# A two-layer streaming encoder: filling products in pieces behind the key tiles, and a second attention that goes tile by tile

## The reference

```python
# layer 0
a_out = gmlp_spatial_gate(...)                      # 1024 wide
b_out = dsa_attention(q, k, v, iq, ik, iw, bias)    # 16 heads of 64, one shared k and v,
                                                    # top-256 keys of those allowed, softmax
mix   = concat([a_out, b_out]) @ w_out              # 2048 x 1024
# layer 1
c_out_heads = swa_sink_attention(q, k, v, sinks, bias)  # 16 heads, 2 key/value heads (8 each),
                                                        # band of two 64-token chunks, sink logit
mix   = c_out_heads @ c_w_out                       # 1024 x 1024
# both layers
h = h + rms_norm(mix, g1)
h = h + rms_norm(squared_relu_mlp(rms_norm(h, g2)), g3)
```

## Time and profile before

| what | value |
|---|---|
| median of 3 runs (from to) | 2545.99 us (2543.73 to 2550.15) |
| span of the profiled execution | 2557.9 us (no other time of that execution is given) |
| TensorE busy | 95% |
| first attention, first to last denominators | 463.18 to 805.51 us |
| second attention, first to last denominators | 1684.85 to 1843.71 us |
| first product of the stage after it | 1910.08 us |

### The profile page before, as it was taken

One profiled execution on the slowest core, in us unless ns is written; L12 is line 12 of the kernel. 1 busy time (PEld: TensorE's weight loads), 2 busy tenths in 40 slices (PEclk: granted clock), 3 DMA queues, 4 the chain that ended last, 5 costly groups with the idle time before them and its releaser, 6 DMA issues.

```text
span 2557.9 us, 34068 instructions
## 1 busy us (share of the span) xinstructions
PE 2427.4 (95%) x11680; PEld 1996.4 (78%) x11680; DVE 1694.0 (66%) x2859; ACT 1183.7 (46%) x2025; POOL 1472.5 (58%) x817
## 2 busy tenths in 40 slices
PE   7899999898998999999999999989989999999997
PEld 5689888777776778888778887867777888878886
DVE  5469998667775486655666676167758655576676
ACT  5442533556664274444333236265555444434331
POOL 2111578645553129887678642357725887578951
PEclk9999999899999999999999999989999999999999
DMA  5380643733544624455644444755553454754343
GB/s 150 63 129 26 134 101 125 238 103 100 157 131 163 214 86 140 140 168 151 238 165 162 141 134 128 169 148 136 133 186 99 146 167 138 240 199 146 115 140 132
DMA packets 324244, 369.64 MB, mean 145 GB/s; under 512 B 13874, under 2 KB 222290, under 8 KB 322052
## 3 DMA queue, kind: packets, MB, share of 16 engines
q1 hardware_dynamic: 315476, 351.96, 47.2%
q10 hardware_dynamic: 8352, 15.21, 2.0%
q0 software_dynamic: 272, 0.62, 0.1%
HBM read 237.18 MB, written 130.55 MB: 144 GB/s over the span
## 4 chain that ended last, share of the span: by engine, by line
PE 75%; DVE 6%; POOL 6%; DMA 4%; issue 4%; ACT 4%; SPq 1%; POOLq 0%; DVEq 0%; ACTq 0%
PE ps L462 72%; PE ps L2675 2%; POOL attn_out_split L1239 1%; POOL attn_out L1237 1%; DMA hidden<-cat_scratch 1%; DMA cat_scratch<-attn_out_split 1%; ACT relu_scores L1508 1%; DVE masks L2068 1%; POOL w_split L417 1%; PE ps L579 1%; DMA h_operand_raw<-h_operand_scratch 1%; POOL attn_out_split L1235 1%; DVE logits L2202 1%; ACT junk L1349 1%; POOL attn_out_low L1232 1%
## 5 line engine op out<-in xcount | busy, mean ns | idle before, releaser
L462 PE MATMUL ps<-xn_T,w_split 128*128 128x512 f32 (+1 forms) x2928 | 679.7, 391 | 2.2 <-ACT x_sums L1386 1.4
L462 PEld LDWEIGHTS ps<-xn_T,w_split 128*128 128x128 f32 (+1 forms) x2928 | 548.6, 188 | 121.2 <-DVE xn_T L2001 2.7
L417 POOL TENSOR_TENSOR w_split<-w_raw,w_split 128x1024 fp32r<-128x1024 f32 x78 | 199.5, 2568 | 484.4 <-ACT w_split L410 484.0
L462 PE MATMUL ps<-w_operand,h_operand 128*128 128x512 f32 x2016 | 461.6, 391 | 11.4 <-DVE acc L2471 7.5
L462 PEld LDWEIGHTS ps<-w_operand,h_operand 128*128 128x128 f32 x2016 | 379.8, 189 | 93.2 <-issue 10.7
L1263 POOL TENSOR_TENSOR w_split<-w_raw,w_split 128x512 fp32r<-128x512 f32 x168 | 242.2, 1454 | 105.5 <-ACT w_split L1766 104.0
L462 PE MATMUL ps<-x_sums_high,w_split 128*128 128x512 f32 x896 | 285.0, 389 | 0.0
L1295 POOL TENSOR_TENSOR w_operand<-w_block,w_operand 128x2048 fp32r<-128x2048 f32 x42 | 207.4, 4938 | 110.9 <-ACT w_operand L1786 110.9
L2473 DVE TENSOR_TENSOR acc<-acc,ps 128x512 f32<-128x512 f32 x288 | 185.4, 680 | 123.7 <-PE ps L462 123.5
L462 PE MATMUL ps<-w_split,hidden 128*128 128x512 f32 x960 | 228.8, 400 | 18.2 <-DMA hidden<-cat_scratch 7.1
L462 PEld LDWEIGHTS ps<-w_split,hidden 128*128 128x128 f32 x960 | 184.8, 194 | 59.5 <-issue 10.6
(11 more groups left out here) (279 smaller groups left out, 4252.0 us busy)
## 6 DMA issues: line engine op xcount, KB each, us to landing
h_operand_raw<-h_operand_scratch SPq DMA_DIRECT2D x42, 1024.0 KB, 5.4
w_raw<-in_w SPq DMA_DIRECT2D x72, 512.0 KB, 8.0
w_block<-in_w SPq DMA_DIRECT2D x48, 512.0 KB, 5.7
q_scratch<-q_split SPq DMA_DIRECT2D x128, 128.0 KB, 2.6
cat_scratch<-attn_out_split SPq DMA_DIRECT2D x128, 128.0 KB, 2.6
w_raw<-in_w_in SPq DMA_DIRECT2D x30, 512.0 KB, 5.4
q_tile<-q_scratch ACTq DMA_DIRECT2D x58, 256.0 KB, 2.7
h_operand_scratch<-h_even SPq DMA_DIRECT2D x14, 1024.0 KB, 4.4
```

Source lines behind the costliest of these rows:

```text
L417: nc.gpsimd.tensor_tensor(whl[:, n0 % 4, 1, :], wraw[:, n0 % 4, :], whl[:, n0 % 4, 0, :].bitcast(F32), ALU.subtract).then_inc(w_lo, 1)
L462: return nc.tensor.matmul(out_ap, stat, mov, start=start, stop=stop)
```

## The change

**First attention.** A fill is cut into four pieces of one weight tile each (three matmuls). A table says how many pieces each step gets, and `piece_places` puts them behind the transposes of the step's last key tiles (for b = 0 and 1 also ahead of them and at the end). Four pieces go ahead of all steps, between the second and third head's logits. The fills are 8 per head group. The second weight group is split in the last step of head group 1, the third in the last step of group 3; a weight buffer is given back piece by piece (`piece_done`). GpSimd makes the low part of weight tile 3 before the mask bias of step 2.

**Second attention.** The steps go over key/value head, query tile, head group: two steps in a row finish half of the input of one token tile. 24 fills instead of 16: k = 32 to 47 in steps 5 to 20, and k = 48 to 55, which are the second half for tiles 0 to 3, in steps 23 to 30, added to `acc`. Their weights are split in steps 21 and 22 by ScalarE and in 22 and 23 by VectorE. Unit tiles are loaded from step 1 on. `pe_out1` does the second half for tiles 4 to 7 only, from unit tiles. The residual rows of tiles 0 to 3 are loaded inside the attention, and the next stage's first weights at step 25.

```diff
-B_F1 = B_O1 + 16
+B_F1 = B_O1 + 8
+STEP1 = [(2 * kv + e, b) for kv in range(2) for b in range(NB) for e in range(2)]
+FILL1 = {g: [32 + g - 5] if 5 <= g < 21 else [48 + g - 23] if 23 <= g < 31 else [] for g in range(HG * NB)}
+FIRST_PIECES = 4
+PIECES = [4, 4, 2, 3, 4, 4, 5, 6]
+PIECES_FIRST = [4, 4, 2, 2, 3, 3, 4, 6]
+PIECES_LAST = [4, 4, 4, 4, 5, 5, 6, 0]
+def piece_places(b, n):
+    if b == 0:
+        return ["pre", "pre", 0, "end"]
+    if b == 1:
+        return ["pre", 0, 1, "end"]
+    return ["pre"] * max(0, n - b - 1) + list(range(max(0, b + 1 - n), b + 1))
...
+def fill_piece(pe, p):
+    k, j = divmod(p, 4)
+    u, half, n = k // 2, k % 2, T_O0 + 4 * (k // 16) + j
+    pe.wait_ge(w_lo, n + 1)
+    if j == 0:
+        pe.wait_ge(fu_ld[u % 2], 32 * (u // 2 + 1))
+        pe.wait_ge(fo_free, k)
+        own_wait(pe)
+    ...
+    mm(ps[:, 7, :], sh, wh, j == 0, False)
+    mm(ps[:, 7, :], sh, wl, False, False)
+    mm(ps[:, 7, :], sl, wh, False, j == 3).then_inc(fo_full if j == 3 else piece_done, 1)
...
             for st in range(keys):
-                if st and st in fills:
-                    fill0(*fills[st])
                 transposes(g, st)
                 if st and todo:
                     logits(g + 1, todo.pop(0))
+                pieces(g, st)
                 if st >= 2:
                     values(g, st - 2)
...
+        for g in range(HG * NB):
+            for k in FILL1[g]:
+                after_fill(k)
+            spill(g)
+            if g == 1:
+                for n in range(T_O1 + 4, T_O1 + 8):
+                    load_tile(sp, n, tile_src(n))
+                for e in range(2):
+                    sp.wait_ge(q_sp[e], 1024)
+            if g in (1, 3):
+                step_pair_spilled(g)
+                fill_units(sp, 1, 16 + g // 2)
...
+            if g == 29:
+                step_pair_spilled(g)
+                unit_tiles(sp, late[:, 0], 1, 6, cat_first)
+                sp.wait_ge(l1_free, 4 * HG * NB)
+                for t in range(2, 4):
+                    load_h(sp, 3, t)
+        step_pair_spilled(HG * NB - 1)
+        unit_tiles(sp, late[:, 1], 1, 7, cat_rest)
...
             probs_low(pL1[:, s, 1, :], ps[:, 4 + q % 2, :], pL1[:, s, 0, :], q)
+            if g in (22, 23):
+                for n in range(T_O1 + 4 + 2 * (g - 22), T_O1 + 6 + 2 * (g - 22)):
+                    weight_low(n)
+            for k in FILL1[g]:
                 take_fill(k)
...
+        for t in range(4, NB - 1):
+            loaded(t)
+            for half in range(2):
+                ...
+                if f >= B_O1 + 4:
+                    pe.wait_ge(b_free, f - 3)
+                for j in range(4):
+                    last = unit(t, half, f, j, j == 0, j == 3)
+                last.then_inc(b_full, 1)
+        transpose_xn(pe, 3, 0, 0, 4)
+        loaded(NB - 1)
```

More of the change, by code:

```diff
@@ L101, with piece_plan @@
 UP_RING = [-3, -3, -2, -2, -1, -1, 0]
[L104 to L120, removed]
+FIRST_PIECES = 4
[8 more added lines that the diff above has]
+    return ["pre"] * max(0, n - b - 1) + list(range(max(0, b + 1 - n), b + 1))
+def piece_plan():
+    plan, done, p = {"start": list(range(FIRST_PIECES))}, {}, FIRST_PIECES
+    for g in range(HG * NB):
+        i, b = divmod(g, NB)
+        plan[g], done[i, b] = {}, [0] if g == 0 else []
+        for place in piece_places(b, (PIECES_FIRST, PIECES, PIECES, PIECES_LAST)[i][b]):
+            plan[g].setdefault(place, []).append(p)
+            if p % 4 == 3:
+                done[i, b].append(p // 4)
+            p += 1
+    assert p == 128
+    return plan, done
+PLAN0, FILL = piece_plan()
 def mask_off(b):
@@ L1166, in pool_program @@
         pool_attn0(pool, mask_bias)
-        pool_out(pool, LAYERS[0])
+        for n in range(T_F0 - 4, T_F0):
+            split_lo(pool, n)
         pool_norm(pool, 1)
@@ L1370, in scale @@
             act.wait_ge(n_rb, 4 * (s - 1) + t // 2 + 1)
+            if s == 3 and t == 0:
+                for e in range(2):
+                    act.wait_ge(o_sp[e], 16 + 1024)
             nc.scalar.activation(xn[:, 0, :, t * P:(t + 1) * P], acc[:, t, :].rearrange("p (k m) -> p k m", k=KT), ACT.Copy,
@@ L1586, in act_program @@
         act_attn0(act)
-        act_out(act, LAYERS[0])
+        for n in range(T_F0 - 4, T_F0):
+            split_hi(act, n)
         norm(1)
@@ L2264, in dve_attn0 @@
                 near(g + 1, j)
-            if fills:
-                take_fill(fills[-1])
+            take_fills(PLAN0[g].get("end", []))
             dve.wait_ge(pv_done, X0[g + 1])
@@ L2694, in values @@
             mm(ps[:, 6, :], vv, pT[:, x % 4, 1, :], False, st == KEYS0[g % NB] - 1).then_inc(pv_done, 1)
-        for j in range(4):
-            logits(0, j)
+        logits(0, 0)
+        logits(0, 1)
+        pieces("start")
+        logits(0, 2)
+        logits(0, 3)
         pe.wait_ge(b_free, B_O0)
@@ L2718, in pe_attn0 @@
                 logits(g + 1, j)
-            if "end" in fills:
-                fill0(*fills["end"])
+            pieces(g, "end")
             if g == 0:
```

400 lines of the change are left out of this document (204 added, 196 removed).

## The result

The changed kernel takes 2561.91 us, median of 4 runs (2556.5 to 2563.52), the kernel before 2545.25 beside it (2543.73 to 2550.15): a ratio of 1.0053 with a 95% interval of 1.0041 to 1.0066. It is slower by half a per cent, and I had forecast 2519. A second set of 7 runs gave 1.0042 (1.0025 to 1.0059).

The account below looks back on a forecast made before the run. TensorE, busy 95% of the span, was taken as the bound, with gains only where it waits. First attention 18.8 us plus second attention and tail 8 make 26.8 us off: 2519 us, range for 8 in 10 2497 to 2545.

Parts of the forecast that it names:

- signs of being wrong: Middle groups staying at 85 us on average, first pieces of fills waiting, or spills pushing the scaling of tile 0.
- Steps 1 to 5, six fills to 4.25 ... Removing 1.75 ... I take 4.2: 46.1.: First attention, middle group: fewer fills would shorten these steps from 50.33 us by 4.2 to 46.1.
- Steps 6 and 7 at 28.6: First attention, middle group: 2.75 fills in eleven pieces would take 28.6 us, against 27.06 read as having none.
- The fourth group "even": First attention, last head group: load kept within a quarter in steps 1 to 4, so no gain or loss.
- Step 0 at 5.8: First attention, middle group: going from none to one fill would take this step from 3.68 to 5.8 us.
- The start, hidden by ScalarE's wait until 474.30: First attention: holding two first logits behind four pieces costs some 4 us, hidden by ScalarE's wait for a transfer.
- one bank for all pieces: Rival, first attention: fills wait for VectorE's copy of the last, 1.5 us each, 46 us: 2565 us, chance 0.08.
- VectorE's loop sets the pace: Rival, first attention: taking fills out of steps 1 to 5 wins nothing; 2538 us, chance 0.2.
- gains nothing: Rival, second attention: unit tile, weight steps and spills ahead of the norm cost their upper ends; 2527 us, chance 0.2.
- The first unit tile: Second attention, step 5: its load lands behind four weight tiles, so TensorE waits 7.5 us, bounds 0 and 12.
- Steps 22 to 24: Second attention: weight splits inside the loop make these steps 20.6 us, between 14.6 and 22.5.
- The tail: From the second attention's last denominators to the next stage's first product: 36.5 us instead of 66.4, 29.9 won.

Follow-up runs that it names:

- the kernel with the last piece behind the denominators: The changed first attention with the second attention of before; from b = 2 on, each step's last piece goes behind the denominators: 1.0015 of the kernel before.
- the plan with whole fills: Kernel before with first attention in pieces behind key tiles, one whole fill in steps 0 to 29, two in step 30, none at the start: 2539.2 us, 0.9966.
- The second profile: The kernel before run once more, unchanged, for another profile: 2548.17 us, 0.9995 of before.
- the spread kernel: First attention of before; changed second attention with unit tiles loaded before weights, high parts a step earlier, low parts one at a time: 2539.01 us, 0.9967 of before.

## Why the prediction was wrong, step by step

**First attention: forecast 18.8 us won; measured 7.9 us lost by the profile** (last denominators at 813.44 for 805.51). By group, from the first to the last, I had forecast 9.9, 0.6, 8.3 and 0 us won; the profile has 0.6, -7.5, 2.4 and -3.5. Two of the signs of being wrong that I had named came: the middle groups stand at 88 us on average, and the first pieces of fills wait.

- *"Steps 1 to 5, six fills to 4.25 ... Removing 1.75 ... I take 4.2: 46.1."* This is the step that failed: 52.1 us. Two errors lie in it, and the kernel with the last piece behind the denominators parts them, since it has the same counts and no wait for the copy in these steps: 48.6 us. Some 0.7 of that is the last piece of step 5, which moves into step 6 (the same move takes 49.5 to 48.8 us in the plan with whole fills). So the fills taken away are worth 1.0 to 1.7 us, not 4.2; in steps 3 and 4 six matmuls fewer save a third of their own time. And the waits cost the other 2.7 to 3.4 us, which I had left out of the sum and put into a rival: counts of 3, 4 and 4 pieces put the beginning of a fill at the last key tile of steps 3, 4 and 5, one key tile behind the end of the last fill, where it waits 0.6 to 1.0 us in front of values and denominators. In the whole attention TensorE waits 12.0 us in 16 places, 0.75 us each. Steps 3 and 4 take 23.1 us with seven pieces in the changed kernel and 21.0 with eight in whole fills.
- *Steps 6 and 7 at 28.6.* They take 31.0. The 27.06 "with none" contained half a fill, and 2.75 fills are three quarters of a fill beyond one in each step: 27.4 and 2.0 (at 2.6 us a fill) are 29.4, and the two waits of 0.6 us make most of the rest.
- *The fourth group "even".* It loses 3.5 us, 1.8 of them in step 6, where six pieces with a wait of 1.4 us take 17.31 us for 15.55.
- *Step 0 at 5.8.* 4.3 and 5.5; right within the 1.5 us that the weight splits move about.
- *The start, hidden by ScalarE's wait until 474.30.* I had put it at some 4 us. The first denominators come 8.9 us later, those of step 2 only 2.7 later: against that execution of before the cover worked in the main. With the rest of the group, which wins 3.3 us where I had 9.9, this leaves 0.6. But the cover isn't always there. Of seven profiles of kernels with the old plan, the copy behind this wait starts in three at 474.30, 473.70 and 474.36, and in the others at 473.29, 472.06, 472.58 and 471.22; step 2 ends at 483.3 to 483.9 with the late transfer and at 479.6 to 481.7 with the earlier one. In three profiles with the changed start it ends at 485.0 to 486.5, so the start costs 3 to 7 us there, an estimate over different executions.
- *The rival "one bank for all pieces"* had 0.08. It was a mechanism at work, at 0.39 us a fill rather than 1.5: only half of the fills began right behind another. Below its own threshold of 1.1 it would not have decided alone; it did so because the 18.8 us weren't there. *"VectorE's loop sets the pace"* (0.2) was right in the main for steps 3 and 4. The two together are what happened, and I had treated them as alternatives, each against a full gain.

**Second attention: forecast 8 us won; measured 1.7 by the profile, nothing by the runs.** That is the rival "gains nothing".

- The first unit tile: 8.3 us of wait for 7.5, right; the step is 15.5 us for 13.6, since its matmuls then run slowly.
- Steps 22 to 24: 26.6 us (1806.02 to 1832.63) instead of 20.6, above my bound of 22.5. This is a term mis-sized by 6. It isn't VectorE's work: I priced the four low parts at 7.9 us, and they take 6.2. I had left out that TensorE stands behind them in a row, and that its clock falls behind the idle time, so that six matmuls of a fill take 2.8 us, twice. I had also read the earlier trace rows too simply: both of its low parts ran beside GpSimd, the shorter one for a part of its time; one that VectorE makes undisturbed takes 1.2 us.
- A late unit tile in step 29 costs 2 us; not foreseen.
- The tail: 36.4 for 36.5. Its idle time of 5.4 us is near the 4 to 5 that I gave it, but it waits for a unit tile, not for the norm. That the sum comes out to 0.1 us is luck: ScalarE's last copy ends 1.3 us behind the denominators, not 2.3, and from there to its last scaling it is 24.2 us, not 22.7.

**From the profile to the median.** I took the 26.8 us from a span of 2557.9 over to a median of 2546, as if the 11.9 us between them were common to both kernels. They weren't. In the later runs of before the time is 1.7 to 1.9 us above the span, so its profiled execution took about 2559.7 us (an estimate), more than any of the 34 runs of before in the second set (2542.21 to 2555.63). The second profile (span 2553.9) is 5.0 us shorter in one later stage alone: 908.80 to 969.64 us is 60.8 us at a mean granted clock of 0.94, in the second profile 55.9 at 1.00. The changed kernel's span is 1.4 below its median. By the profiles' spans alone the change costs 2.6 us, by the medians of the runs 16.7 and, in the second set, 10.2. Part of that gap is the transfer of step 2 above, which came late in both profiles of before. Where the rest lies in the timed executions isn't shown.

What stays open: the exact price of the four pieces at the start (0.07%, within the intervals), and why the whole-fill plan wins 0.34% beyond before; the price by step would explain it (one fill a step, one step with two, where before has up to two a step), but I ran no kernel that changes only that. Why a wait for the copy costs little in steps with eight pieces and more than its length at the end of steps with four is open too.

## What to carry to other kernels

Price a filling product step by step, by cutting some of its matmuls in one kind of step and looking at that step's length. A line between "none" and "many" hides the corner at which fills stop being cheap, and the step with "none" must really have none. When fills share one bank, leave room between the end of one and the beginning of the next: the place of a last piece hardly matters by itself, but a handshake at the end of a step holds up everything behind it. And a wait that covers new work must be looked at in several profiles before it is counted on.

## What the runs showed of the hardware

- In the spread kernel the granted clock fell to its lower level behind idle times of 1.4 us (with a shorter one of 0.6 us and a little work ahead of it) and 1.7 us, not only behind the 3.4 us of the changed kernel. The 1 us windows show 0.50 from 1792 to 1795 and from 1799 to 1802, while TensorE was busy again. Six matmuls of 512 columns take 1.6 us at full clock and 2.7 to 2.9 at the lower one.
- VectorE's low part of a weight tile (128 x 1024, two inputs) takes 1.22 us in two places of the spread kernel and 1.84 and 2.22 in the other two, and GpSimd's operation beside it stretches too, as these rows of VectorE and GpSimd show:

```profile
1792.98 1.22 DVE L2349 TENSOR_TENSOR w_split<-w_raw,w_split 128x1024 fp32r<-128x1024 f32 x1
...
1795.55 2.22 DVE L2349 TENSOR_TENSOR w_split<-w_raw,w_split 128x1024 fp32r<-128x1024 f32 x1
```

```profile
1793.13 1.53 POOL L1259 COPY attn_out_low<-attn_out 64x512 f32<-64x512 f32 x1 [1.07 <-DVE attn_out L2344]
...
1795.42 1.26 POOL L1264 TENSOR_TENSOR attn_out<-attn_out,attn_out_split 64x512 f32<-64x512 f32 x1
1796.76 2.14 POOL L1266 TENSOR_TENSOR attn_out_split<-attn_out,attn_out_low 64x512 fp32r<-64x512 f32 x1
```

GpSimd's copy takes 0.61 us and the sum of 1796.76 about 1.28 elsewhere. The Trainium skill (SBUF — State Buffer, Who interferes with whom) has the two engines exclude each other for such operands; the trace agrees. The price goes by order: at 1792.98 VectorE comes first and GpSimd's copy is the longer one; at 1795.42 GpSimd comes first, VectorE's low part of 1795.55 is the longer one, and GpSimd's next sum, begun at 1796.76 within it, again.
